# Reordering around the seams of a transformer block: masks, taps, scaled queries, readout, entry turns, tail rows

## Chip, cores and metric

The kernel runs on one core of one Trainium2 chip, as one program. The metric is the device time in microseconds, lower is better. The names of the engines are TensorE (PE, weight loads PEld), VectorE (DVE), ScalarE (ACT), GpSimd (POOL) and SyncE (SP), whose queue issues nearly all transfers.

## The reference

A transformer block on 1024 latent rows and 256 context rows of width 1024, all in float32:

```python
def _ffn_sublayer(x, shift, scale, gate, w13, w2, g, b):
    y = _swiglu(_modulate(x, shift, scale), w13, w2)
    return _layer_norm(ALPHA * x + FFN_RES * gate * y, g, b)

def reference(x, c, ctx, ...):
    ml = silu(c) @ w_ada + b_ada            # nine rows: shifts, scales, gates
    x_lat = _ffn_sublayer(x, ml[0], ml[1], ml[2], ...)
    x_ctx = _ffn_sublayer(ctx, mc[0], mc[1], mc[2], ...)
    y_lat = _token_mixer(_modulate(x_lat, ml[3], ml[4]), _modulate(x_ctx, mc[3], mc[4]), ...)
    x_lat = _layer_norm(ALPHA * x_lat + ml[5] * y_lat, ...)
    return _ffn_sublayer(x_lat, ml[6], ml[7], ml[8], ...)
```

The token mixer projects both inputs with w_in (the slices q, k, v, o and gates of an mLSTM with 4 heads of 128, and q, k, v of a banded attention with 8 heads of 64 and 2 key-value heads). q and k of the mLSTM go through a depthwise convolution of five taps and a silu. The mLSTM runs in both directions and starts from the states that the context leaves. Its result h is read out as `layer_norm_per_head(h) * g * sigmoid(o)`. The attention sees its own block and the neighbouring ones and the context, with a sink. Both results side by side are multiplied by w_out. The output is the latent rows.

## The kernel before, in words

**Products.** Each float32 operand is split into a high and a low part in the reduced format fp32r, and a product is three matmuls (high by high, low by high, high by low) that accumulate in PSUM. ScalarE makes the high part, VectorE or GpSimd the low one by a subtraction.

**Order.** Each engine's stream is written by hand, in the order of the code; engines meet at semaphores. Nothing is scheduled by a program, except that the projection's steps are cut over the attention's pairs by shares (PAIR_STEPS, below). In the order of the span: modulation and entry, the first FFN, the projection of the context and of a part of the latent rows, the mixed stage (1025 to 1305 us), the mLSTM's cores (to 1377), the output stage (to 1478), the second FFN and, in its last products, the rows of the output (to the end).

**Mixed stage.** 32 pairs of attention heads run between the steps of the projection groups 43 to 81 (mixed_pe; a step is three matmuls, a group eight steps). For a pair p TensorE turns the probabilities (L2483, after VectorE's scaling L2473), makes the next pair's scores, then this pair's values (pair_values_pe, L2505) and then the projection steps PAIR_STEPS[p]. share_cut gives each of the first 12 pairs a share of 1, the last LAST_SHARE, and the others an equal part of what is left. Before, the last pair has 17 steps and finishes groups 79, 80 and 81. In pairs 0 to 3 and 28 to 31 the probabilities are turned in two stages (turn_stages). The groups' results leave PSUM through the convolution's taps: ScalarE makes the first (L2143), VectorE the other four (L2156). After the pairs ScalarE makes the silus of k (L2169, four) and of q (L2928, four), and loads the table for it.

**Decay tiles.** The mLSTM's decays are 16 tiles of 128x512. SyncE loads a tile (L2605), GpSimd masks it (decay_mask_pool, L2636), ScalarE takes exponentials (decay_tile_act, L2628), SyncE stores it (L2611) and loads the third after it, one or two tiles a pair (decays_in). GpSimd also makes the low parts of the weights of units 6 and 7 among these masks (proj_low_pool, L2003, two instructions each) at the places in LOW_AT, and the loads of the next weights (p_raw, L1907), on SyncE's queue, wait for them.

**Cores.** TensorE runs 16 steps of 24 matmuls (L3078): eight with the state and the scaled queries q_rows, eight that update the state, eight with vext and the probabilities d_rows. SyncE loads q_rows and d_rows (rows_sp, L2800 and L2801) into six slots, row j when the last matmuls of step j-6 are done. GpSimd multiplies q_rows by the queries (scaled, L2836) and the scores by d_rows (probabilities, L2844), in the order scaled(i), probabilities(i). Ahead of the loop it makes weighted values and decayed states (weighted_pool L2886, decay_state_pool L2892), which the states of the context wait for.

**Readout.** In the last steps and behind them, for each of eight tiles: VectorE's statistics (L2975, L2982) and two small operations (L2985, L2986), GpSimd's power and product (invert_pool, L2870, L2873), ScalarE's scaling (L2922, four), GpSimd's gating (gated_pool, L2879), TensorE's turn (L3312).

**Output stage.** TensorE makes the w_out products in two halves of the columns. After tiles 5 and 6 of the second half it turns the normed rows 0 to 3 for the first product of the second FFN (L331), four of the eight column blocks each time. ScalarE reads each turn with two instructions (half_act, L358 and L360) and makes the norm of each row (norm_act, L1641). L875 is the first matmul of the second FFN.

**Tail.** The output's layer norm is made row tile by row tile, n = 0 to 7 (out_rows_dve, L3487 centring, L3495 affine). For row n = 6 only the centring is VectorE's; ScalarE scales (row_scaled_act, L3475) and GpSimd adds (L3424). ScalarE makes the sums of a row (L3447 to L3454), GpSimd the power (L3420). Of the last row VectorE makes the statistics (L3458 to L3465) after the last products' gate (L1584) and addition (L1593).

## Time and profile before

| | us |
|---|---|
| median of three runs | 2128.68 |
| the three runs | 2127.88, 2128.68, 2131.55 |
| the profiled execution's own time | 2129.62 |
| its span | 2127.8 |
| TensorE busy | 2091.4 (98%) |
| VectorE busy | 1527.0 (72%) |
| ScalarE busy | 905.6 (43%) |
| GpSimd busy | 192.8 (9%) |

The profile is one execution. The span runs from its first instruction to its last, the time has what lies around it as well. A row of a timeline is a start in us from the span's start, a length in us, the engine, the line of the kernel, the operation and its tiles, the number of instructions joined in the row, and in brackets how long the engine was idle before and what released it. Instructions of one engine are pipelined, so a row may begin before the one ahead of it ends; a matmul's end is modelled.

### The profile page before, as it was taken

Reading aid. Unit: us, or ns where it says so; the run is one execution under the profiler, and the core shown is the slowest. Engines: PE = TensorE matmul, PEld = TensorE weight load, DVE = VectorE, ACT = ScalarE, POOL = GpSimd, SP = SyncE. Lnnn points to the kernel's source line nnn. Section 1 sums busy time; section 2 is a strip of 40 time slices with the busy share of each in tenths; the row PEclk is TensorE's granted clock in tenths of the full one; section 3 lists DMA queues with packets and bytes.
Section 4 is the critical chain, followed back from the end, with each engine's and each line's share of the span. In section 5 each row is a group of like instructions: output and inputs, shape, how many; then the busy total and the mean of one; then the engine's idle time right before and its main releaser. Section 6 shows DMA issues by size and latency. Waiting matters only on the chain.

```text
span 2127.8 us, 31643 instructions
## 1 busy us (share of the span) xinstructions
PE 2091.4 (98%) x11508; PEld 1768.0 (83%) x11510; DVE 1527.0 (72%) x2520; ACT 905.6 (43%) x1631; POOL 192.8 (9%) x212
## 2 busy tenths in 40 slices
PE   8999999999999999999999999999999999999998
PEld 4888888888888888899878878877888888888886
DVE  5778888777648878675665465866867777767787
ACT  4622222222237446542565555734532323336445
POOL 0000000000000001090111002821000000000001
PEclk9999999999999999999999999999999999999999
DMA  8144444555459664733231002732244434349773
GB/s 298 33 142 147 149 134 129 160 167 159 129 186 348 193 215 148 209 101 117 74 108 41 21 21 66 182 109 99 75 134 140 136 104 153 123 139 341 257 234 112
DMA packets 261841, 310.38 MB, mean 146 GB/s; under 512 B 19350, under 2 KB 164686, under 8 KB 261710
## 3 DMA queue, kind: packets, MB, share of 16 engines
q1 hardware_dynamic: 261422, 308.52, 45.4%
q8 instruction: 80, 1.31, 0.2%
q14 instruction: 51, 0.42, 0.1%
q10 hardware_dynamic: 288, 0.13, 0.0%
HBM read 242.13 MB, written 66.45 MB: 145 GB/s over the span
## 4 chain that ended last, share of the span: by engine, by line
PE 86%; DVE 4%; DMA 3%; ACT 2%; issue 1%; POOL 1%; SPq 1%; DVEq 0%; POOLq 0%; ACTq 0%
PE psum L1327 11%; PE psum L1328 11%; PE psum L1329 11%; PE psum L1527 6%; PE psum L1529 6%; PE psum L1528 6%; PE psum L2056 3%; PE psum L2058 3%; PE psum L2057 3%; PE psum L1347 2%; PE psum L1346 2%; PE psum L1345 2%; PE psum L3078 2%; PE psum L875 2%; PE psum L876 2%; PE psum L877 2%
## 5 line engine op out<-in xcount | busy, mean ns | idle before, releaser
L1327 PE MATMUL psum<-x_mix_h,x_op_h 128*128 128x512 f32 x640 | 251.2, 393 | 1.3 <-DVE v_sum L1135 1.2
L1328 PE MATMUL psum<-x_mix_l,x_op_h 128*128 128x512 f32 x640 | 249.8, 390 | 0.0
L1329 PE MATMUL psum<-x_mix_h,x_op_l 128*128 128x512 f32 x640 | 249.5, 390 | 0.0
L1527 PE MATMUL psum<-s_high 128*128 128x512 f32 x616 | 240.0, 390 | 0.3 <-DVE s_low L1514 0.3
L1528 PE MATMUL psum<-s_low,s_high 128*128 128x512 f32 x616 | 239.9, 389 | 0.0
L1529 PE MATMUL psum<-s_high,s_low 128*128 128x512 f32 x616 | 239.9, 389 | 0.0
L1514 DVE TENSOR_TENSOR s_low<-s_raw,s_high 128x1024 fp32r<-128x1024 f32 x154 | 186.9, 1217 | 50.5 <-ACT s_high L1475 50.5
L1475 ACT ACTIVATE s_high<-s_raw 128x1024 fp32r<-128x1024 f32 x154 | 161.3, 1057 | 124.1 <-PE psum L1529 56.3
L1019 ACT ACTIVATE x_op_h<-raw 128x512 fp32r<-128x512 f32 x140 | 86.1, 627 | 203.6 <-PE psum L1329 121.1
L1019 ACT ACTIVATE x_op_h<-w_sum 128x512 fp32r<-128x512 f32 x160 | 97.1, 625 | 162.9 <-DVE w_sum L997 107.1
L1327 PEld LDWEIGHTS psum<-x_mix_h,x_op_h 128*128 128x128 f32 x640 | 120.4, 188 | 25.4 <-issue 1.8
L1329 PEld LDWEIGHTS psum<-x_mix_h,x_op_l 128*128 128x128 f32 x640 | 120.2, 188 | 25.3
L1328 PEld LDWEIGHTS psum<-x_mix_l,x_op_h 128*128 128x128 f32 x640 | 120.4, 188 | 23.2
L1527 PEld LDWEIGHTS psum<-s_high 128*128 128x128 f32 x616 | 115.7, 188 | 24.5 <-DVE s_low L1514 0.8
L1529 PEld LDWEIGHTS psum<-s_high,s_low 128*128 128x128 f32 x616 | 115.7, 188 | 24.2
L1528 PEld LDWEIGHTS psum<-s_low,s_high 128*128 128x128 f32 x616 | 115.7, 188 | 23.9
L1025 DVE TENSOR_TENSOR x_op_l<-raw,x_op_h 128x512 fp32r<-128x512 f32 x140 | 92.8, 686 | 39.2 <-ACT x_op_h L1019 37.0
L2056 PE MATMUL psum<-p_wh,xh_lat 128*128 128x256 f32 x384 | 111.7, 291 | 0.0
L2057 PE MATMUL psum<-p_wl,xh_lat 128*128 128x256 f32 x384 | 108.8, 283 | 0.0
L2058 PE MATMUL psum<-p_wh,xl_lat 128*128 128x256 f32 x384 | 108.8, 283 | 0.0
L1025 DVE TENSOR_TENSOR x_op_l<-w_sum,x_op_h 128x512 fp32r<-128x512 f32 x160 | 107.5, 683 | 0.0
L773 DVE SCALAR_TENSOR_TENSOR ada_sums<-ada_slice,more,ada_sums 128x512 f32<-128x512 f32 x140 | 99.6, 746 | 3.7 <-DVE ada_sums L773 0.5
(408 smaller groups left out, 5069.6 us busy)
## 6 DMA issues: line engine op xcount, KB each, us to landing
raw<-in_ffn_w SPq DMA_DIRECT2D x88, 512.0 KB, 5.4
f_terms<-g_half SPq DMA_DIRECT2D x154, 256.0 KB, 2.3
s_raw<-f_terms SPq DMA_DIRECT2D x154, 256.0 KB, 3.2
s_raw<-in_ffn_w SPq DMA_DIRECT2D x154, 256.0 KB, 4.0
ada_slice<-in_w_ada SPq DMA_DIRECT2D x112, 256.0 KB, 3.1
c_raw<-in_ffn_w SPq DMA_DIRECT2D x22, 512.0 KB, 3.5
p_raw<-in_w_in SPq DMA_DIRECT2D x22, 512.0 KB, 4.0
early<-in_w_ada SPq DMA_DIRECT2D x16, 512.0 KB, 6.6
```

Source lines behind the costliest of these rows:

```text
L1019: nc.scalar.activation(op_tiles(F, op)[0][:], OP_SOURCE[op], ACT.Copy).then_inc(F.hi, 1)
L1025: nc.vector.tensor_tensor(low[:], OP_SOURCE[op], high[:].bitcast(F32), ALU.subtract).then_inc(F.lo, 1)
L1327: nc.tensor.matmul(o, wh[:, k], high(k), start=i < 4 and k == 0, stop=False, skip_group_check=i > 3)
L1328: nc.tensor.matmul(o, wh[:, k], low(k), start=False, stop=False, skip_group_check=i > 3)
L1329: last = nc.tensor.matmul(o, wl[:, k], high(k), start=False, stop=k == KH - 1, skip_group_check=i > 3)
L1514: nc.vector.tensor_tensor(S.low[s % RING][:], S.raw[s % RAWS][:], S.high[s % RING][:].bitcast(F32), ALU.subtract)\
L1527: nc.tensor.matmul(o, h[:, 0, rows], h[:, 1], start=i == 0 and q in (0, 1, 6), stop=False, skip_group_check=True)
L1528: nc.tensor.matmul(o, h[:, 0, rows], l[:, 1], start=False, stop=False, skip_group_check=True)
L1529: return nc.tensor.matmul(o, l[:, 0, rows], h[:, 1], start=False, stop=i == PAIRS - 1, skip_group_check=True)
L2056: nc.tensor.matmul(o[:, 0:w], high, high_w[:, k, :], start=k == 0, stop=False)
L2057: nc.tensor.matmul(o[:, 0:w], high, low_w[:, k, :], start=False, stop=False)
L2058: last = nc.tensor.matmul(o[:, 0:w], low, high_w[:, k, :], start=False, stop=k == KD - 1)
```

## The change

- Masks: the low parts of units 6 and 7 stand one decay mask later on GpSimd (before mask 3 in place of 2, before mask 10 in place of 9).
- Last taps: LAST_SHARE is 1.75 in place of 2.5: the last pair has 12 steps and finishes groups 80 and 81; group 79 is done one pair earlier, and the five steps go to pairs 12 to 30 (pair 12 has 13 in place of 12). ScalarE makes group 79's first tap behind the first of the four silus of k, and group 80's behind the second.
- Values: in the pairs with two turn stages, two steps of the projection stand ahead of the values (three in the last, as before).
- Row loads of the cores need unit 9's group done, in place of all groups.
- Scaled queries: GpSimd scales rows 0 to 3 ahead of the loop, between the weighted values, and row i+4 behind probabilities(i).
- Readout: VectorE's two small operations (a step of its own semaphore with them) go to GpSimd, as two tensor_scalar, with one more semaphore step in front of the power.
- Entry turns: three column blocks after tile 5, three after 6, two after 7, in place of four and four after 5 and 6; so on VectorE and ScalarE, whose norms of rows 5 and 6 stand between.
- Tail: the row whose scaling and addition are ScalarE's and GpSimd's is n = 5 in place of 6; row 6 is VectorE's, and the statistics of the last row's first half are made ahead of it.

```diff
--- before.py
+++ after.py
@@ -2536,7 +2536,7 @@
...
-        FIRST_PAIRS, LAST_SHARE = 12, 2.5
+        FIRST_PAIRS, LAST_SHARE = 12, 1.75
...
@@ -2569,15 +2569,12 @@
...
                     score_pair_pe(pe, p + 1)
-                    pair_values_pe(pe, p)
...
                     pe.wait_ge(rope_kept, len(ROPED))
-                if p + 1 < ATT_PAIRS:
-                    groups_pe(pe, PAIR_STEPS[p])
-                else:
-                    groups_pe(pe, PAIR_STEPS[p][:3])
-                    pair_values_pe(pe, p)
-                    groups_pe(pe, PAIR_STEPS[p][3:])
+                ahead = 3 if p + 1 == ATT_PAIRS else 2 if len(turn_stages(p)) == 2 else 0
+                groups_pe(pe, PAIR_STEPS[p][:ahead])
+                pair_values_pe(pe, p)
+                groups_pe(pe, PAIR_STEPS[p][ahead:])
...
@@ -2669,11 +2666,13 @@
...
             keep_pair_act(act, ATT_PAIRS - 1)
-            silu_k_act(act, range(1, 3))
+            done = groups_done(ATT_PAIRS - 1)
+            silu_k_act(act, range(1, 2))
+            group_act(act, done[0])
+            silu_k_act(act, range(2, 3))
...
             silu_k_act(act, range(3, 4))
-            done = groups_done(ATT_PAIRS - 1)
-            for j in done[:-1]:
+            for j in done[1:-1]:
...
@@ -2776,8 +2775,7 @@
...
             pool.wait_ge(gate_dve, 7)
-            LOW_AT = {2: POOL_LOW[0],
-                      decays_in(next(p for p in range(ATT_PAIRS) if first_of(6) in groups_done(p))).stop: POOL_LOW[1]}
+            LOW_AT = {3: POOL_LOW[0], decays_in(HIGH_IN[POOL_LOW[1]]).stop: POOL_LOW[1]}
...
@@ -2801,7 +2799,7 @@
...
         def mlstm_sp(sp):
-            sp.wait_ge(p_ready, len(GROUPS))
+            sp.wait_ge(p_ready, unit_last(9) + 1)
...
@@ -2848,12 +2846,16 @@
...
                 weighted_pool(pool, n)
+            scaled(0)
+            scaled(1)
...
                 decay_state_pool(pool, n)
+                scaled(n)
             for i in range(LAST):
-                scaled(i)
                 probabilities(i)
+                if i + LAT0 < LAST:
+                    scaled(i + LAT0)
...
@@ -2865,11 +2867,15 @@
...
         def invert_pool(pool, q):
-            _, rate, offset = read_slots(q)
+            mv, rate, offset = read_slots(q)
+            by_head = mv.rearrange("p (h c) -> p h c", c=2)
             pool.wait_ge(read_measured, q + 1)
+            nc.gpsimd.tensor_scalar(offset, by_head[:, :, 0], -1.0, None, op0=ALU.mult)
+            nc.gpsimd.tensor_scalar(rate, by_head[:, :, 1], LN_EPS, None, op0=ALU.add).then_inc(read_inverted, 1)
+            pool.wait_ge(read_inverted, 3 * q + 1)
...
                 .then_inc(read_inverted, 1)
-            pool.wait_ge(read_inverted, 2 * q + 1)
+            pool.wait_ge(read_inverted, 3 * q + 2)
...
@@ -2916,7 +2922,7 @@
...
             _, rate, offset = read_slots(q)
-            act.wait_ge(read_inverted, 2 * q + 2)
+            act.wait_ge(read_inverted, 3 * q + 3)
...
@@ -2969,8 +2975,9 @@
...
             st = small[:, 8:32]
-            mv, rate, offset = read_slots(q)
-            by_head = mv.rearrange("p (h c) -> p h c", c=2)
+            mv, _, _ = read_slots(q)
+            if q:
+                dve.wait_ge(read_measured, q)
...
@@ -2980,11 +2987,7 @@
...
                 last = nc.vector.bn_aggr(mv[:, 2 * h:2 * h + 2], st[:, 6 * h:6 * h + 6])
-            core_step(dve, last)
-            unit = ones.to_broadcast([P, M_HEADS])
-            nc.vector.scalar_tensor_tensor(offset, by_head[:, :, 0], -1.0, unit, op0=ALU.mult, op1=ALU.mult)
-            nc.vector.scalar_tensor_tensor(rate, by_head[:, :, 1], LN_EPS, unit, op0=ALU.add, op1=ALU.mult)\
-                .then_inc(read_measured, 1)
+            last.then_inc(read_measured, 1)
...
@@ -3159,6 +3162,7 @@
...
         MIX = [(0, t) for t in TILES_BACK] + [(1, t) for t in range(TL)]
+        T3_PARTS = {5: range(3), 6: range(3, 6), 7: range(6, KD)}
...
@@ -3238,11 +3242,9 @@
...
             norm_act(act, N2, 4, 4)
-            half_act(act, F2, T3, T3_BANKS, 0, range(4))
-            norm_act(act, N2, 5, 5)
-            half_act(act, F2, T3, T3_BANKS, 0, range(4, KD))
-            norm_act(act, N2, 6, 6)
-            norm_act(act, N2, 7, 7)
+            for t in range(5, TL):
+                half_act(act, F2, T3, T3_BANKS, 0, T3_PARTS[t])
+                norm_act(act, N2, t, t)
...
@@ -3285,10 +3287,8 @@
...
                     first_low(dve, F2)
-                if (half, t) == (1, 5):
-                    half_dve(dve, F2, T3, 0, range(4))
-                if (half, t) == (1, 6):
-                    half_dve(dve, F2, T3, 0, range(4, KD))
+                if half and t in T3_PARTS:
+                    half_dve(dve, F2, T3, 0, T3_PARTS[t])
...
@@ -3363,11 +3363,8 @@
...
                 last.then_inc(mix_ready, 1)
-                if (half, t) == (1, 5):
-                    for k in range(4):
-                        turn_pe(pe, T3, T3_BANKS, norm2_done, (0, k))
-                if (half, t) == (1, 6):
-                    for k in range(4, KD):
+                if half and t in T3_PARTS:
+                    for k in T3_PARTS[t]:
...
@@ -3378,6 +3375,7 @@
...
         LAST_ROWS = list(range(4, TL)) + list(range(4))
+        SPLIT_ROW = TL - 3
...
@@ -3402,10 +3400,10 @@
...
             for n, t in enumerate(LAST_ROWS[:-1]):
-                if n < TL - 2:
-                    sp.wait_ge(out_affined, n + 1)
+                if n == SPLIT_ROW:
+                    sp.wait_ge(row_added, ADDED_BEFORE + 1)
                 else:
-                    sp.wait_ge(row_added, ADDED_BEFORE + 1)
+                    sp.wait_ge(out_affined, n + int(n < SPLIT_ROW))
...
@@ -3419,7 +3417,8 @@
...
                     .then_inc(N1.inverted, 1)
-                if n == TL - 2:
+                if n == SPLIT_ROW + 1:
+                    t = LAST_ROWS[SPLIT_ROW]
...
@@ -3469,9 +3468,9 @@
...
-            t = LAST_ROWS[TL - 2]
+            t = LAST_ROWS[SPLIT_ROW]
             act.wait_ge(row_centred, CENTRED_BEFORE + 1)
-            act.wait_ge(N1.inverted, 2 * TA + TL - 1)
+            act.wait_ge(N1.inverted, 2 * TA + SPLIT_ROW + 1)
...
@@ -3486,7 +3485,7 @@
...
                                                          op0=ALU.add, op1=ALU.mult)
-                if n == TL - 2:
+                if n == SPLIT_ROW:
...
@@ -3532,13 +3531,12 @@
...
                 if t == 3:
+                    half_sums_dve(dve, 3, 1)
...
                     out_rows_dve(dve, 4 + t - 1)
-                if t == 2:
-                    half_sums_dve(dve, 3, 1)
...
```

ScalarE at the end of the attention, from the load of the silu's table; L2169 is a silu of k, L2143 a first tap, L2928 (after the change L2934) a silu of q, L2495 and L2513 the last pair's turned probabilities and rows. Before:

```order
L2169 ACT_TABLE_LOAD
L2169 ACTIVATE kT<-kT,more 128x1280
L2495 ACTIVATE late_pT<-psum 128x512
L2495 ACTIVATE pair_pT<-psum 128x512
L2169 ACTIVATE kT<-kT,more 128x1280 x2
L2513 ACTIVATE qaT<-psum 128x128
L2169 ACTIVATE kT<-kT,more 128x1280
L2143 ACTIVATE qT<-psum,more 128x510
L2143 ACTIVATE qT<-psum,more 128x512
L2928 ACTIVATE qT<-qT,more 128x1024 x3
L2143 ACTIVATE qT<-psum,more 128x510
```

With the change:

```order
L2169 ACT_TABLE_LOAD
L2169 ACTIVATE kT<-kT,more 128x1280
L2143 ACTIVATE qT<-psum,more 128x510
L2495 ACTIVATE late_pT<-psum 128x512
L2495 ACTIVATE pair_pT<-psum 128x512
L2169 ACTIVATE kT<-kT,more 128x1280
L2143 ACTIVATE qT<-psum,more 128x512
L2169 ACTIVATE kT<-kT,more 128x1280
L2513 ACTIVATE qaT<-psum 128x128
L2169 ACTIVATE kT<-kT,more 128x1280
L2934 ACTIVATE qT<-qT,more 128x1024 x3
L2143 ACTIVATE qT<-psum,more 128x510
```

The two first taps that stood behind the fourth silu of k (groups 79 and 80) are now behind the first and the second of them. The three silus of q stand ahead of the last tap in both.

GpSimd at the start of the mLSTM's cores; w_v are weighted values, q_rows the scaled queries, d_rows the probabilities. Before:

```order
L2886 TENSOR_TENSOR w_v<-vext,tok_gate 128x516 [waits p_ready,p_read_act]
L2886 TENSOR_TENSOR w_v<-vext,tok_gate 128x516
L2886 TENSOR_TENSOR w_v<-vext,tok_gate 128x516 [waits update_ready]
L2892 TENSOR_TENSOR state<-state,decay_all 128x516 [waits state_done]
L2886 TENSOR_TENSOR w_v<-vext,tok_gate 128x516 [waits update_ready]
L2892 TENSOR_TENSOR state<-state,decay_all 128x516 [waits state_done]
L2836 TENSOR_TENSOR q_rows<-q_rows,qT 128x512 [waits silu_done,q_gate_in]
L2844 TENSOR_TENSOR d_rows<-scores,d_rows 128x512 [waits sc_kept,d_in]
L2836 TENSOR_TENSOR q_rows<-q_rows,qT 128x512 [waits rope_in]
L2844 TENSOR_TENSOR d_rows<-scores,d_rows 128x512 [waits gate_in]
```

With the change:

```order
L2892 TENSOR_TENSOR w_v<-vext,tok_gate 128x516 [waits p_ready,p_read_act]
L2892 TENSOR_TENSOR w_v<-vext,tok_gate 128x516
L2834 TENSOR_TENSOR q_rows<-q_rows,qT 128x512 [waits silu_done,q_gate_in]
L2834 TENSOR_TENSOR q_rows<-q_rows,qT 128x512 [waits rope_in]
L2892 TENSOR_TENSOR w_v<-vext,tok_gate 128x516 [waits update_ready]
L2898 TENSOR_TENSOR state<-state,decay_all 128x516 [waits state_done]
L2834 TENSOR_TENSOR q_rows<-q_rows,qT 128x512 [waits q_gate_in]
L2892 TENSOR_TENSOR w_v<-vext,tok_gate 128x516 [waits update_ready]
L2898 TENSOR_TENSOR state<-state,decay_all 128x516 [waits state_done]
L2834 TENSOR_TENSOR q_rows<-q_rows,qT 128x512 [waits rope_in]
L2842 TENSOR_TENSOR d_rows<-scores,d_rows 128x512 [waits sc_kept,d_in]
L2834 TENSOR_TENSOR q_rows<-q_rows,qT 128x512 [waits q_gate_in]
```

Four scaled rows moved ahead of the first probabilities; from then on a row is scaled four steps before its own probabilities.

VectorE in the tail, from the centring of row 5; L1584 and L1593 are gate and addition of a 512-wide product, L3458 (L3457) statistics of half a row. Before:

```order
L3487 SCALAR_TENSOR_TENSOR y<-y,out_stats,ln_rows_286 128x1024
L3495 SCALAR_TENSOR_TENSOR y<-y,out_stats,ln_rows_286 128x1024
L3458 BN_STATS out_stats<-y 128x6
L3487 SCALAR_TENSOR_TENSOR y<-y,out_stats,ln_rows_286 128x1024
L1584 TENSOR_TENSOR s_sums<-psum,gate_row_278 128x512
L1593 SCALAR_TENSOR_TENSOR y<-y,s_sums 128x512
L3458 BN_STATS out_stats<-y 128x6
```

With the change:

```order
L3486 SCALAR_TENSOR_TENSOR y<-y,out_stats,ln_rows_286 128x1024
L3457 BN_STATS out_stats<-y 128x6
L3486 SCALAR_TENSOR_TENSOR y<-y,out_stats,ln_rows_286 128x1024
L3494 SCALAR_TENSOR_TENSOR y<-y,out_stats,ln_rows_286 128x1024
L1584 TENSOR_TENSOR s_sums<-psum,gate_row_278 128x512
L1593 SCALAR_TENSOR_TENSOR y<-y,s_sums 128x512
L3457 BN_STATS out_stats<-y 128x6
```

Of row 5 only the centring is left here, the statistics moved ahead of row 6, and row 6 has both its instructions ahead of the last gate.

## Rows read from the trace of the kernel before

**Rows 1.** The page's part 1: busy us, share of the span, instructions.
```profile
PE 2091.4 (98%) x11508; PEld 1768.0 (83%) x11510; DVE 1527.0 (72%) x2520; ACT 905.6 (43%) x1631; POOL 192.8 (9%) x212
```

**Rows 2.** Waits of TensorE, 1000 to 1500 us: total, times, longest.
```profile
PE psum L2483 <- DVE att_p L2473: 6.4, 5, 3.2
...
PE psum L3312 <- POOL y_m L2879: 1.2, 2, 0.6
...
PE psum L331 <- ACT x_quarter L360: 0.9, 2, 0.7
...
PE psum L2505 <- ACT pair_pT L2495: 0.6, 2, 0.3
```

**Rows 3.** Windows: length, busy time by engine, granted clock, DMA share, bandwidth.
```profile
1090.00:1100.00 10.00, 6.81 (x52) 5.05 (x51) 4.79 (x10) 4.99 (x15) 2.29 (x3) 1.00 0.64 184
...
1300.00:1310.00 10.00, 8.01 (x29) 6.13 (x28) 6.00 (x8) 6.02 (x8) 0.00 (x0) 0.83 0.00 0
...
1360.00:1375.00 15.00, 11.11 (x83) 10.76 (x81) 13.58 (x44) 9.01 (x27) 12.08 (x13) 0.89 0.15 41
```

**Rows 4.** Timelines by unit 7: start, length, engine, line, operation, idle time before.
```profile
1086.78 4.75 POOL L2003 TENSOR_TENSOR p_wl<-p_raw,p_wh 128x1024 fp32r<-128x1024 f32 x2 [10.20 <-ACT p_wh L1985]
...
1089.19 2.73 SPq L1907 DMA_DIRECT2D p_raw<-in_w_in  x2
...
1095.81 1.31 PE L2483 MATMUL psum<-ident,att_p 128*128 128x128 f32 x10 [3.19 <-DVE att_p L2473]
...
1100.49 1.28 ACT L2628 ACTIVATE d_stage<-d_stage,tok_gate 128x128 f32<-128x128 f32 x4 [2.69 <-POOL d_stage L2636]
```

**Rows 5.** Timelines of GpSimd and TensorE by unit 6.
```profile
1040.45 4.73 POOL L2003 TENSOR_TENSOR p_wl<-p_raw,p_wh 128x1024 fp32r<-128x1024 f32 x2 [9.20 <-ACT p_wh L1985]
...
1057.92 1.09 PE L2483 MATMUL psum<-ident,att_p 128*128 128x128 f32 x8 [1.50 <-DVE att_p L2473]
```

**Rows 6.** Timelines of ScalarE and TensorE, end of attention.
```profile
1304.15 3.21 ACT L2928 ACTIVATE qT<-qT,more 128x1024 f32<-128x1024 f32 x3
...
1305.52 0.59 PE L2047 MATMUL psum<-xh_lat,p_wh 128*128 128x512 f32 x1 [1.99 <-DVE qT L2156]
...
1318.04 1.16 PE L3063 MATMUL psum<-qT,kT 128*128 128x128 f32 x8 [0.30 <-ACT qT L2928]
```

**Rows 7.** Loop: timelines, a window of TensorE, landings of q_rows.
```profile
1359.92 3.55 DVE L2985 SCALAR_TENSOR_TENSOR small<-small,consts 128x4 f32<-128x4 f32 x1
...
1362.18 1.27 POOL L2844 TENSOR_TENSOR d_rows<-scores,d_rows 128x512 f32<-128x512 f32 x1
...
1365.89 1.13 PE L3078 MATMUL psum<-state,q_rows 128*128 128x129 f32 x8 [3.81 <-issue]
...
1375.20 1.13 PE L3078 MATMUL psum<-state,q_rows 128*128 128x129 f32 x8 [0.28 <-issue]
...
1340.00:1360.00 20.00, 19.68 (x175) 19.52 (x176) 1.00 0.93 241
...
DMA to landing us min/median/max: 3.5/4.3/5.9
```

**Rows 8.** Timeline of GpSimd, readout.
```profile
1403.00 0.20 POOL L2873 TENSOR_TENSOR small<-small 128x4 f32<-128x4 f32 x1
...
1404.97 1.29 POOL L2879 TENSOR_TENSOR y_m<-y_m,o_in 128x512 f32<-128x512 f32 x1 [1.77 <-ACT y_m L2922]
```

**Rows 9.** Timelines of ScalarE and TensorE, entry turns.
```profile
1478.28 1.32 ACT L1641 ACTIVATE y<-y,ln_stats 128x1024 f32<-128x1024 f32 x1
...
1478.52 0.50 PE L875 MATMUL psum<-xh_lat,f_h 128*128 128x512 f32 x1 [0.37 <-ACT x_quarter L360]
```

**Rows 10.** Timelines of VectorE and GpSimd, tail.
```profile
2119.24 0.69 DVE L1593 SCALAR_TENSOR_TENSOR y<-y,s_sums 128x512 f32<-128x512 f32 x1
...
2121.18 2.28 DVE L3487 SCALAR_TENSOR_TENSOR y<-y,out_stats,ln_rows 128x512 f32<-128x512 f32 x2
...
2119.51 2.62 POOL L3424 TENSOR_TENSOR y<-y,ln_rows 128x1024 f32<-128x1024 f32 x1 [2.15 <-ACT y L3475]
```

## The prediction, made before the changed kernel ran

> **What bounds the kernel now.** I began with the page: TensorE is busy for 98% of the span [rows 1], so only its pauses, its slow clock and what stands ahead of its first and behind its last matmul can give or cost time. Next the waits of TensorE from 1000 to 1500 us [rows 2], where all of the change but its last part lies: 6.4 us before the turns L2483, 1.2 before L3312, 0.9 before L331, 0.6 before L2505; a pause of 3.81 in the mLSTM loop, put down to no releaser, comes on top [rows 7]. Then the granted clock [rows 3]: 1.00 at 1090 to 1100, although a pause of 3.19 us lies in it; 0.83 at 1300 to 1310; 0.89 at 1360 to 1375. Ten us at 0.83 lack 1.7 us of work at 2.4 GHz, fifteen at 0.89 also 1.7. Each of these two falls to 1.2 GHz lies about a pause (1.99 and 3.81 us, [rows 6, 7]). Then the timelines of the four engines at each place.
>
> **The sum** is made against the profiled execution: span 2127.80, its own time 2129.62. The median of the runs is 2128.68, 0.94 lower, so 0.94 is taken off at the end.
>
> **A. Mask ahead of the low parts of unit 6: 0.** GpSimd sat idle 9.20 us before that low part, released by ScalarE's high part at 1040.45 [rows 5]. One mask more ahead of it finds its rows not yet loaded or an idle engine. The low part still waits for ScalarE, and the pause of 1.50 behind it stays.
>
> **B. The same for unit 7: -0.3.** Before: GpSimd's low parts take 4.75 us from 1086.78, the mask stands behind them, ScalarE's decay exponentials, queued ahead of the softmax, come late, and TensorE waits 3.19 at 1095.81 [rows 4]. With the mask first this pause goes. But SyncE issues the decay tile's store and the next load behind p_raw's two loads, which wait for the low parts (2.73 us from 1089.19). That queue isn't changed: the next tile's mask still waits for a load, so its exponentials (they stood 2.69 us idle at 1100.49 [rows 4]) come late one pair further on. Behind that pair TensorE waits about 2.9 instead of 3.19. Bounds: -3.2 (no pause returns) and +1.7 (the same pause, with a fall of the clock).
>
> **C. Last taps, LAST_SHARE 1.75: -3.9.** At 1305.52 TensorE waits 1.99 for VectorE's taps [rows 6], and these wait for ScalarE's first tap, which stood behind all four silus of kT. Now that tap stands behind one silu, the next behind two, and group 79 is done a pair earlier: the pause goes (-2.0), and with it the fall of the clock in that stretch (-1.7). The five steps that leave the last pair fill others: of the five pauses at L2483 (6.4), those of 3.19 and 1.50 leave 1.7 for three, and larger pairs lie at two of these: -0.9. Against it: the three silus of qT (3.21 us [rows 6]) now stand right ahead of group 81's tap on ScalarE, which comes about 1 us later as the group is done sooner after them; the wait of 0.30 for the last silu at 1318.04 becomes 1.0: +0.7. Bounds -4.7 and -2.0.
>
> **D. Values two steps later in seven pairs: +0.4.** The two pauses it aims at are 0.6 together [rows 2]. They lie in pairs 0 and 1, ahead of the 1.50 of A, which is set by a chain of GpSimd and ScalarE: what is saved ahead of it is waited for there. What stays is one more switch between projection and values in each pair. Bounds 0 and +1.0.
>
> **E. Scaled queries four ahead, small operations off VectorE: -4.0.** TensorE's longest pause, 3.81 at 1365.89, has VectorE's L2985 as its cause: an operation on 128x4 elements that took 3.55 us while GpSimd ran its instructions of 1.27 us without a gap [rows 7]. L2985 is gone: -3.8, and the fall of clock behind it, -1.7. What it costs: GpSimd now runs probabilities(i+1) behind scaled(i+4), which needs row i+4. SyncE issues that row when the matmuls of step i-2 are done. A step has 24 matmuls and 175 ran in 20 us [rows 7]: 2.7 a step. From there to the start of step i+1's last 8 matmuls are 3 x 2.7 - 1.0 = 7.1 us; two GpSimd instructions, 2.5, leave 4.6 for the row's landing. The rows land in 3.5 to 5.9, 4.3 in the middle [rows 7]; the long ones are those of the loop's start, where weights load beside them. Before, the same scaling had five steps. Writing the loop out step by step with these numbers, its end moves from 1375.6 (clock at 2.4 GHz throughout) to 1371.9 with all landings at 3.5, 1372.6 at 4.3, 1374.7 at 5.1, 1377.9 at 5.9. I take 1373.1, since one or two rows will be late and the others not: against the profile (the last step begins at 1375.20 [rows 7] and ends 1.9 later, 1377.1) -4.0. Bounds -5.2 and +0.8.
> The row says that one VectorE instruction waited for three of GpSimd in a row. The Trainium skill (SBUF — State Buffer, Who interferes with whom) has an exclusive lock for a VectorE instruction with two SBUF inputs against a GpSimd instruction that reads SBUF, held by the first to issue for its whole instruction; by that the wait would be one instruction, 1.2, and E would bring 2.4 less, since the rest of the 3.81 would have another cause. The trace disagrees with it in length: 3.55 is nearly three times 1.27.
>
> **F. Readout: +1.2.** Two tensor_scalar of 128x4 and one more semaphore step now stand on GpSimd in the chain statistics, power, product, ScalarE, gating. TensorE waited for the end of that chain (1.2 at L3312 [rows 2]), and so did GpSimd for ScalarE (1.77 before the last gating [rows 8]), so the chain's length counts whole. A 128x4 product there takes 0.20 [rows 8]; two of them and a step more, less the two that leave VectorE, I put at 0.4 a tile over the last three tiles. Bounds 0.6 and 1.8.
>
> **G. Entry turns in threes: +1.0.** ScalarE's two last parts went on until L875 at 1478.52; the norm of row 6 came behind them, 1.32 from 1478.28 [rows 9]. It now stands ahead of the last two turns: +1.3, and the second FFN starts so much later. Of the 0.9 at L331 [rows 2] 0.3 goes. Bounds 0 and 1.8. TensorE's idle time gathers in one piece of about 3 us ahead of L875, a place where the clock may fall.
>
> **H. Tail: +1.5.** Before, row 6's addition on GpSimd (2.62 from 2119.51) held VectorE's L3487: two halves 2.28, of which 1.4 is their work, and the last L3495 began right behind it, at 2123.5 [rows 10]. Now row 5 goes to GpSimd, and its addition comes when ScalarE has scaled it, which it does after the sums of row 6: about 2117.95. VectorE is then in row 6's L3495 (until about 2118.8, as it must wait for its power). GpSimd's addition follows, 2118.8 to 2121.2, and VectorE's L1593, two SBUF inputs, which was at 2119.24, gets held until 2121.2: +2.0. The 0.9 of holding at L3487 is gone, the last power now comes up while L3487 holds the way: +0.1 to +0.7. Bounds +0.3 (the two never meet) and +2.6 (GpSimd gets in first, row 6's L3495 waits for it, and PSUM-reading L1584 too).
> The Trainium skill (SBUF — State Buffer, Who interferes with whom) says that a VectorE instruction with one SBUF input doesn't contend; by that L1584 passes. No row above shows it, and the sum holds both.
>
> Sum: 0 - 0.3 - 3.9 + 0.4 - 4.0 + 1.2 + 1.0 + 1.5 = -4.1. There are three places with a new or remaining pause of 1.3 to 3 us (turns of the pair behind unit 7, loop start, ahead of L875). A pause of 1.99 had a fall and one of 3.19 had none, so the pause alone doesn't decide; I expect one fall, +1.7. 2129.62 - 4.1 + 1.7 - 0.94 = **2126.3**.
>
> **Rivals.**
> 1. *The gains stand, no fall* (chance 0.25). For: both falls of before lie at pauses that go. 2126.3 - 1.7 = 2124.6; with landings at 3.5 to 4.3 (-0.9) and a harmless tail (-1.2) 2122.5.
> 2. *Unit 7's pause doesn't return* (0.10): the store after unit 7 finds the queue free early enough. 2126.3 - 2.9 = 2123.4.
> 3. *The row's landing becomes the loop's bound, slower* (0.14). At 1329 to 1339 weights, rows and gates load together, and the landing of 5.9 is from there. The point is 4.6; from it each us costs some 4. With 5.9 throughout, +4.8: 2131.1; with the several pauses in one stretch a second fall, +1.7: 2132.8; with the tail at its worst, +1.1: 2133.9. Against: rows later in the loop landed in 3.5 to 4.3.
> 4. *Two or more falls* in the new pauses (0.06): 2128.1 to 2129.9.
> The change does what it says in the order of the instructions, so no rival is made of that.
>
> **Numbers.** The forecast has 0.45, with its own range 2124.4 to 2129. About 0.2% (4.3 us) is what a measurement can tell from no change: 2124.4 to 2132.9. Faster: rivals 1 and 2, and 0.03 of the forecast, 0.38. Slower: two thirds of rival 3, 0.10. The rest, 0.52, is within. The range reaches from rivals 1 and 2 with a part of the low bounds, 2120.5, to rival 3, 2132.5.
>
> **What will show it.** B: a wait of about 2.9 before L2483 at 1101 to 1104 and none at 1096. C: no wait before L2047 near 1304, clock 1.00 there, a wait of about 1 before L3063. E: no L2985; the waits of TensorE in the loop's first eight steps, behind L2842 (probabilities), and q_rows' landings against 4.6. F: the gatings of the last tiles 0.4 further apart on GpSimd. G: the norm of row 6 ahead of the last two turns, L875 about 1.3 later behind row 5's norm, idle in one piece. H: VectorE's L1593 held until GpSimd's addition ends. I am wrong if the loop's end, counted from its first L3078, doesn't come at least 2 us earlier, or if a part that I cost at nothing (A) shows a pause.

## The result

The changed kernel takes **2141.86 us** (median of five runs, 2138.93 to 2144.56), the kernel before 2129.17 in the same comparison. One of the five runs of before took 4236.48 us; the ratio is made without it. The ratio is 1.0059, 95% interval 1.0047 to 1.0070: slower by 12.6 us. The forecast was 2126.3, its range 2120.5 to 2132.5; the chance given to a loss was 0.10.

The profiled execution of the changed kernel took 2142.53 us, its span is 2140.4. I cut both spans at the starts of eight rows that both traces have, and take the differences:

| stage, from one start to the next | before | changed | difference |
|---|---|---|---|
| up to the first turn L2483 of the mixed stage (not edited) | 1031.8 | 1030.0 | -1.8 |
| mixed: to the scores' wait (L3063, now L3066) | 286.2 | 283.5 | -2.7 |
| cores: to their last eight matmuls (L3078, now L3081) | 58.1 | 62.0 | +3.9 |
| readout: to the turn of tiles 5 to 7 (L3312) | 30.2 | 37.8 | +7.6 |
| output stage: to L875 | 72.1 | 74.5 | +2.4 |
| second FFN: to the last matmul | 639.6 | 640.8 | +1.3 |
| tail: to the last affine operation (L3495, now L3494) | 5.4 | 7.7 | +2.3 |
| its outputs | 4.3 | 3.9 | -0.4 |

**Profile after.** TensorE's part of the page, and its waits from 1000 to 1500 us, which answer to [rows 1, 2]:

```profile
PE 2096.9 (98%) x11508; PEld 1773.2 (83%) x11510; DVE 1524.0 (71%) x2504; ACT 907.1 (42%) x1631; POOL 197.9 (9%) x228
...
PE psum L3312 <- POOL y_m L2885: 5.9, 2, 3.5
PE psum L3081 <- POOL d_rows L2842: 5.7, 3, 2.6
PE psum L2483 <- DVE att_p L2473: 5.0, 3, 2.7
PE psum L875 <- ACT x_quarter L360: 3.3, 1, 3.3
...
PE psum L3066 <- ACT qT L2934: 1.2, 1, 1.2
```

The share is still 98%, and nothing in the page tells of a loss of 12 us; the waits do. L3312 went from 1.2 us to 5.9, the loop's matmuls wait 5.7 for probabilities, and one pause of 3.3 stands ahead of L875. Of the waits of before, those at L2505, L331 and L2047 are gone.

The windows around the pauses (length, busy times, granted clock, DMA share, GB/s), which answer to [rows 3]:

```profile
1100.00:1110.00 10.00, 7.25 (x48) 5.72 (x48) 7.00 (x13) 7.79 (x24) 1.27 (x2) 0.83 0.43 139
1330.00:1345.00 15.00, 12.47 (x97) 12.28 (x96) 9.72 (x23) 11.59 (x35) 11.59 (x9) 0.89 0.76 209
1352.00:1367.00 15.00, 11.89 (x89) 11.70 (x90) 9.21 (x36) 8.97 (x30) 11.39 (x10) 0.89 0.46 135
1385.00:1395.00 10.00, 7.61 (x40) 6.72 (x39) 3.70 (x18) 5.13 (x12) 3.50 (x7) 0.83 0.15 47
1408.00:1420.00 12.00, 8.47 (x39) 6.82 (x37) 6.23 (x11) 6.76 (x11) 3.25 (x5) 0.86 0.33 86
1485.00:1495.00 10.00, 7.10 (x24) 5.71 (x25) 3.86 (x9) 4.09 (x6) 1.13 (x2) 0.83 0.26 105
```

Each of the six stretches has a fall to 1.2 GHz: 10 us at 0.83, 12 at 0.86 and 15 at 0.89 lack 1.7 us each, the same step as before. With one near 40 us there are seven before the last matmul; the profile of before has three (near 40 too, and the two of [rows 3]). Between these two executions four more falls of 1.7 are 6.8 of the 12.6 us. Over all runs it is less. The mean granted clock was 0.9934 in the five runs of the changed kernel and 0.9950 in the 64 runs of the kernel before that were made beside the experiments, which lack 14.1 and 10.7 us. By that estimate 3 of the 12.6 us are clock, about two falls; the profile of before was one with few.

### The profile page after: what moved, and what is told of

Its sections match the earlier page's. It is cut to its first block, busy times and chain, and to the rows that moved or that the text cites. A ratio compares the mean times of both kernels' runs of the same rounds, so it can differ in the third digit from the quotient of the medians.

```text
span 2140.4 us, 31650 instructions
## 1 busy us (share of the span) xinstructions
PE 2096.9 (98%) x11508; PEld 1773.2 (83%) x11510; DVE 1524.0 (71%) x2504; ACT 907.1 (42%) x1631; POOL 197.9 (9%) x228
## 4 chain that ended last, share of the span: by engine, by line
PE 89%; DMA 3%; POOL 2%; ACT 2%; DVE 2%; issue 1%; SPq 1%; DVEq 0%; POOLq 0%; ACTq 0%
PE psum L1328 12%; PE psum L1327 12%; PE psum L1329 12%; PE psum L1527 6%; PE psum L1529 6%; PE psum L1528 6%; PE psum L2056 3%; PE psum L2058 3%; PE psum L2057 3%; PE psum L1347 2%; PE psum L1346 2%; PE psum L1345 2%; PE psum L875 2%; PE psum L876 2%; PE psum L877 2%; PE psum L2483 1%
## 5 line engine op out<-in xcount | busy, mean ns | idle before, releaser
L1634 POOL TENSOR_TENSOR ln_stats<-ln_stats,consts 128x1 f32<-128x1 f32 x18 | 15.5, 863 | 950.8 <-DVE ln_stats L1629 950.8
```

## The experiments

Each kernel's stages, cut as above, in us of its profiled execution, and its median and ratio to the kernel before with the 95% interval:

| kernel | mixed | cores | readout | output | FFN | tail | median | ratio |
|---|---|---|---|---|---|---|---|---|
| before | 286.2 | 58.1 | 30.2 | 72.1 | 639.6 | 5.4 | 2129.2 | |
| changed | 283.5 | 62.0 | 37.8 | 74.5 | 640.8 | 7.7 | 2141.9 | 1.0059 [1.0047, 1.0070] |
| e1 | 285.9 | 56.4 | 34.4 | 74.6 | 639.2 | 7.7 | 2135.5 | 1.0031 [1.0019, 1.0042] |
| e2 | 285.7 | 61.9 | 30.4 | 73.8 | 640.8 | 7.7 | 2137.9 | 1.0039 [1.0025, 1.0052] |
| e3 | 285.3 | 61.1 | 37.4 | 72.7 | 639.6 | 7.7 | 2141.7 | 1.0062 [1.0045, 1.0079] |
| e4 | 286.1 | 60.8 | 37.8 | 74.6 | 640.8 | 5.4 | 2140.5 | 1.0054 [1.0034, 1.0075] |
| e5 | 285.3 | 59.2 | 36.2 | 73.8 | 640.6 | 7.8 | 2140.5 | 1.0057 [1.0040, 1.0073] |
| e6 | 286.7 | 60.9 | 36.2 | 75.7 | 639.3 | 7.7 | 2139.5 | 1.0045 [1.0029, 1.0062] |
| e7 | 284.4 | 59.1 | 30.3 | 72.1 | 639.6 | 5.4 | 2127.4 | 0.9994 [0.9985, 1.0004] |
| e8 | 286.0 | 58.1 | 30.8 | 72.2 | 640.0 | 5.4 | 2128.9 | 0.9998 [0.9989, 1.0008] |
| e9 | 286.1 | 58.1 | 30.2 | 72.2 | 639.6 | 5.4 | 2127.1 | 0.9987 [0.9978, 0.9997] |
| e10 | 284.0 | 54.2 | 31.2 | 72.1 | 639.7 | 5.4 | 2121.9 | 0.9961 [0.9948, 0.9974] |
| e11 | 285.5 | 55.4 | 37.5 | 74.3 | 640.8 | 7.7 | 2137.9 | 1.0038 [1.0026, 1.0050] |
| e12 | 285.3 | 60.4 | 36.1 | 75.7 | 639.2 | 7.8 | 2141.4 | 1.0061 [1.0043, 1.0078] |
| e13 (one run) | 285.0 | 55.7 | 31.1 | 72.1 | 639.6 | 5.4 | 2125.0 | |
| e14 | 285.2 | 54.1 | 31.1 | 72.1 | 639.6 | 5.4 | 2124.1 | 0.9973 [0.9962, 0.9985] |
| e15 | 282.9 | 54.3 | 30.9 | 72.1 | 639.7 | 5.4 | 2120.6 | 0.9964 [0.9950, 0.9978] |

Runs of one kernel lie 2 to 10 us apart, so an edit of 2 us is read from its stage, not from the medians.

**e1: scaled queries not ahead.**

```diff
-            scaled(0)
-            scaled(1)
...
-                scaled(n)
             for i in range(LAST):
+                scaled(i)
                 probabilities(i)
-                if i + LAT0 < LAST:
-                    scaled(i + LAT0)
```

> The changed kernel with GpSimd's order in the cores as before: scaled(i) right ahead of probabilities(i), none four ahead. Measured from the first score matmul (L3066) to the start of the last eight matmuls of the cores this stage took 58.1 us before and 62.0 with the change. Theory (the row's landing became the loop's bound, since probabilities(i+1) stands behind the scaling of row i+4): the three waits for probabilities (2.5, 0.5, 2.6) and the fall of the clock behind them go, and since VectorE's L2985 is no longer there either, the stage takes 53 to 55 and the whole time falls by 7 to 9 us against the changed kernel (2141.9). Rival (SyncE's queue and the load beside it: the rows are loaded earlier, so the weights' loads fall differently): the order on GpSimd doesn't matter, the stage stays at 60 to 63.

The cores take 56.4, 5.6 less than in the changed kernel, and the median falls by 6.3. The waits for probabilities are gone, so the theory's mechanism holds and the rival (60 to 63) does not; the theory's sizes, 53 to 55 and 7 to 9 us, were both missed. What is missing is a new wait, for scaled queries at 1370, where GpSimd's longer readout operations stand ahead of them, with a fall of the clock at it:

```profile
1370.08 2.06 PE L3077 MATMUL psum<-state,q_rows 128*128 128x129 f32 x8 [2.68 <-POOL q_rows L2834]
```

The changed kernel's rows show what e1 took away. GpSimd, SyncE's queue, TensorE and the landings of q_rows:

```profile
1334.12 1.27 POOL L2834 TENSOR_TENSOR q_rows<-q_rows,qT 128x512 f32<-128x512 f32 x1 [3.35 <-DMA q_rows<-gate_rows]
...
1355.51 1.27 POOL L2834 TENSOR_TENSOR q_rows<-q_rows,qT 128x512 f32<-128x512 f32 x1 [3.07 <-DMA q_rows<-gate_rows]
...
1327.63 1.76 SPq L1913 DMA_DIRECT2D p_raw<-in_w_out  x2
1329.50 0.54 SPq L2798 DMA_DIRECT2D q_rows<-gate_rows  x1
...
1346.40 1.28 SPq L1913 DMA_DIRECT2D p_raw<-in_w_out  x2
1347.78 0.54 SPq L2798 DMA_DIRECT2D q_rows<-gate_rows  x1
...
1336.67 1.16 PE L3081 MATMUL psum<-vext,d_rows 128*128 128x129 f32 x8 [2.53 <-POOL d_rows L2842]
...
1358.05 1.66 PE L3081 MATMUL psum<-vext,d_rows 128*128 128x129 f32 x8 [2.62 <-POOL d_rows L2842]
...
DMA to landing us min/median/max: 3.5/4.0/7.7
```

Two rows of the ten that are issued in the loop do most of it, and both stand right behind loads of weights (p_raw) on SyncE's queue. Row 6 could have gone when step 0's last matmul ended, at 1327.0, but is issued at 1329.50 and lands 4.5 later: 7.0 in all against the budget of 4.6, and TensorE waits 2.53. Row 12 is issued at 1347.78, 0.3 after its slot was free, and lands 7.7 later, the longest landing. GpSimd, with the probabilities of an earlier step queued behind it, stands idle 3.07 and scales it at 1355.51, and TensorE waits 2.62. This is rival 3, down to its budget. The six other kernels that scale four ahead (e2 to e6, e12) repeat it: row 6 stands behind weights in all of them, and TensorE waits 2.0 to 2.7 us there; row 12 lands 6.0 to 7.9 after its issue.

**e2: the readout's small operations on VectorE again.**

```diff
-            nc.gpsimd.tensor_scalar(offset, by_head[:, :, 0], -1.0, None, op0=ALU.mult)
-            nc.gpsimd.tensor_scalar(rate, by_head[:, :, 1], LN_EPS, None, op0=ALU.add).then_inc(read_inverted, 1)
-            pool.wait_ge(read_inverted, 3 * q + 1)
...
+            core_step(dve, last)
+            nc.vector.scalar_tensor_tensor(offset, by_head[:, :, 0], -1.0, unit, op0=ALU.mult, op1=ALU.mult)
+            nc.vector.scalar_tensor_tensor(rate, by_head[:, :, 1], LN_EPS, unit, op0=ALU.add, op1=ALU.mult)
```

> The changed kernel with the two small operations of the readout on VectorE again (two scalar_tensor_tensor behind a step), GpSimd having power and product alone. From the start of the last eight matmuls of the cores to the last turn of the readout (L3312, 12 matmuls) it took 30.2 us before and 37.8 with the change. Theory (each of eight tiles has two more GpSimd operations and a semaphore round in a chain that TensorE waits for, 0.7 to 1.2 us a tile, and the late third tile delays ScalarE's gate rows and with them the next): this stage falls to 30 to 32, with 1 to 2.5 us on top in TensorE's clock. In the cores' stage L2985 is back and may again stand behind GpSimd's instructions for 1 to 3.6 us, so that of the 6 to 7 us up to 3.6 are lost there. Rival (the readout is late because the cores end late and ScalarE's other work stands in the way): the stage stays above 35.

The readout takes 30.4 in place of 37.8: theory. The median falls by 4.0 only; 1.7 of the 7.4 is a fall of the clock that this profile of the changed kernel has in the stage. The chain of one tile in the changed kernel, on GpSimd:

```profile
1400.57 1.30 POOL L2885 TENSOR_TENSOR y_m<-y_m,o_in 128x512 f32<-128x512 f32 x1 [1.77 <-ACT y_m L2928]
1401.95 0.56 POOL L2873 TENSOR_SCALAR small<-small 128x4 f32<-128x4 f32 x1
1402.57 0.53 POOL L2874 TENSOR_SCALAR small<-small 128x4 f32<-128x4 f32 x1
1403.19 1.04 POOL L2876 TENSOR_TENSOR small<-small,consts 128x4 f32<-128x4 f32 x1
1404.30 0.20 POOL L2879 TENSOR_TENSOR small<-small 128x4 f32<-128x4 f32 x1
1406.27 1.29 POOL L2885 TENSOR_TENSOR y_m<-y_m,o_in 128x512 f32<-128x512 f32 x1 [1.77 <-ACT y_m L2928]
```

From gating to gating it is 5.70 us; before, the same two gatings were 4.75 apart (1400.22 to 1404.97, the later one in [rows 8]). The two tensor_scalar take 0.56 and 0.53 while VectorE runs its low parts, and 0.23 each at 1388.7 to 1389.3, where VectorE is idle. L2985 (L2987 in this kernel) met no row of GpSimd's instructions (it took 0.16 to 0.88); the order on GpSimd is another here, which is likely the reason; the loss of 1 to 3.6 us in the cores that I allowed for did not come, and the cores' 61.9 are e1's matter.

**e3: entry turns in fours**, T3_PARTS = {5: range(4), 6: range(4, KD)} and ScalarE's order with it.

> The changed kernel with the entry turns in fours again. From the last readout turn to L875 it took 72.1 us before and 74.5 with the change, and the first 12 us of the second FFN ran at a granted clock of 0.86. Theory (the norm of row 6 ahead of the last two turns on ScalarE makes one idle stretch of 3.3 us, and the clock falls behind it): the pause before L875 falls from 3.3 to 0.4 to 0.6, the clock behind it is 1.00, and the time falls by 2.5 to 4.5 us against the changed kernel. Rival (the pause only gathers what lies at other places otherwise): L331 gets its 0.9 back and two thirds of the gain are gone, below 1.5 us.

The pause before L875 is gone (changed: 3.27 at 1487.90, with a clock of 0.83 behind it in the window above), the output stage is 1.8 shorter and the FFN 1.2: 3.0 us by the profile, as the theory has it. The median moved by 0.2 only, which is the rival's size. The four runs had a lower clock on average, 0.9922 against 0.9934, which is 2.5 us, so the medians don't decide. Nor is the 3.0 all certain: eight profiles have the pause of 3.3 (3.25 to 3.27), and a fall stands behind it in five (changed, e2, e4, e5, e11) and not in e1, e6 and e12.

**e4: the tail as before**, SPLIT_ROW = TL - 2, the half's statistics back in their place.

> The changed kernel with the tail as before: row 6 is the one that is scaled by ScalarE and added by GpSimd. From the last matmul to the last affine operation (L3494) it took 5.4 us before and 7.7 with the change, in which row 6's L3494 took 3.3 us beside GpSimd's addition. Theory: the stage is 5.4 again, 2.3 us less. Rival (the delay came from elsewhere, as from ScalarE's sums being later): it stays above 7.

5.4 again: theory. What the exchange did, VectorE and GpSimd in the changed kernel:

```profile
2129.03 3.28 DVE L3494 SCALAR_TENSOR_TENSOR y<-y,out_stats,ln_rows 128x1024 f32<-128x1024 f32 x1 [0.50 <-POOL out_stats L3418]
2132.23 0.68 DVE L1584 TENSOR_TENSOR s_sums<-psum,gate_row 128x512 f32<-128x512 f32 x1
2132.94 0.69 DVE L1593 SCALAR_TENSOR_TENSOR y<-y,s_sums 128x512 f32<-128x512 f32 x1
...
2134.89 1.54 DVE L3486 SCALAR_TENSOR_TENSOR y<-y,out_stats,ln_rows 128x512 f32<-128x512 f32 x2
...
2127.45 1.47 POOL L3418 TENSOR_TENSOR out_stats<-out_stats,consts 128x1 f32<-128x1 f32 x1 [5.08 <-ACT out_stats L3453]
2128.89 2.34 POOL L3423 TENSOR_TENSOR y<-y,ln_rows 128x1024 f32<-128x1024 f32 x1
```

GpSimd's addition and VectorE's L3494 both want to start at 2129, as both come behind the power L3418; GpSimd goes first (2.34 us), L3494 takes 3.28 in place of the 1.28 of a row of that size, and everything behind it, the last gate L1584 first, is 2 us late. L3486 of the last row gets 0.7 back (1.54 in place of 2.28 [rows 10]).

**e5: masks as before**, LOW_AT with 2 and 9.

> The changed kernel with only the masks' places as before (low parts of units 6 and 7 ahead of masks 2 and 9). From the first turn of the mixed stage to the first scores of the last head (the wait for silu of q) the kernel before took 286.2 us; the changed kernel and four variants of it took 283.5 to 286.1, all with a wait of 2.6 to 2.8 near 1102 and matmuls at half the clock behind it. Theory (the pause only moved, and at its new place the clock falls, which it did not before): with the masks back the pause is 3.2 near 1094 again, the clock there is 1.00, and the stage takes 282 to 283.5. Rival (the masks' move changes nothing by itself; the clock falls there because of the values' or shares' move): the stage stays at 284.5 to 286, with a granted clock below 1.00 between 1090 and 1110.

The pause is 3.20 at 1096.46 again and the clock there is 1.00, but a fall stands near 1058 in its place, at the pause behind unit 6's masks, which nobody touched. The stage is 285.3, within the rival's bounds and outside the theory's. Neither holds: this pointed to chance, which e13 then tested.

**e6: values as before**, the two steps ahead of them only in the last pair.

> The changed kernel with the values right behind the next pair's scores again in pairs 0 to 3 and 28 to 30. Theory (switches of 0.4 in all, swallowed or not): the mixed stage changes by less than 1 us (284 to 286). Rival (in these pairs the values two steps later delay ScalarE's copy of the pair's rows and so the turns): 1 to 3 us less, 282 to 283.5.

286.7 with three falls (5.1). Without pauses (the scores' wait among them) and falls the stage has a rest of 273.2 us, against 275.1 in the changed kernel. The ten profiles with the values moved have 274.7 to 275.2, the seven without 273.1 to 273.7. (The figures up to 276.4 in the expectation of e9 left the scores' wait in.) TensorE in pair 28 of the changed kernel, from two steps to values and back:

```profile
1283.22 0.50 PE L2047 MATMUL psum<-xh_lat,p_wh 128*128 128x512 f32 x1
1283.56 0.40 PE L2048 MATMUL psum<-xl_lat,p_wh 128*128 128x512 f32 x1
...
1284.50 0.39 PE L2049 MATMUL psum<-xh_lat,p_wl 128*128 128x512 f32 x1
1284.82 0.66 PE L2505 MATMUL psum<-pair_pT,va 128*64 128x128 f32 x8
...
1285.85 0.50 PE L2047 MATMUL psum<-xh_lat,p_wh 128*128 128x512 f32 x1
1286.18 0.40 PE L2048 MATMUL psum<-xl_lat,p_wh 128*128 128x512 f32 x1
```

Matmuls of a projection start 0.23 apart. Behind a switch it is 0.34 (1283.22 to 1283.56), ahead of the values 0.32. No pause is shown for it. Pairs 28, 29 and 30 lasted 8.21, 7.53 and 8.22 from turn to turn, and 7.96, 7.27 and 7.95 here: 0.26 a pair, 1.8 for seven. The theory said less than 1 and the rival 1 to 3 by a later copy; the rest moves by 1.9, the rival's size by another way. The stage as a whole, 286.7, is outside both ranges because of its three falls.

**e7: the attention's parts alone**, all behind it as before.

> The kernel before with the attention's parts alone: masks, LAST_SHARE with the last taps, values; rows, scaled queries, readout, entry turns and tail as before. Theory (the loss of 12 us lies in cores, readout, entry and tail): the mixed stage as in the changed kernel (283.5 to 286), cores 58, readout 30 and tail 5.4 as before, so the time is 2127 to 2130. Rival (the last taps' new order makes the scores' wait of 1.2 and carries it into the cores): the cores' stage is 1 to 2 us longer than 58.1 and the time is 2130 to 2132.

2127.4, readout and tail as before. The cores' one microsecond more is in the clock: behind the same pause of 3.81 (now at 1361) 3.4 us are lost, not 1.7. The loss of 12 us lies in cores, readout, entry and tail.

**e8: e7 with one-input operations.**

```diff
-            nc.vector.scalar_tensor_tensor(offset, by_head[:, :, 0], -1.0, unit, op0=ALU.mult, op1=ALU.mult)
+            nc.vector.tensor_scalar(offset, by_head[:, :, 0], -1.0, None, op0=ALU.mult)
```

> The same, and the two small operations of the readout, on VectorE, are tensor_scalar with one SBUF input (mean by -1, variance plus epsilon) in place of scalar_tensor_tensor with a second input of ones. Theory (the 3.55 us of L2985 came from its second SBUF input, which goes through what GpSimd holds): the operation takes 0.2 to 0.3, the pause of 3.8 in the cores and the clock's fall behind it go, cores 53 to 55 in place of 58, time 2122 to 2126. Rival (any VectorE operation that reads SBUF waits there while GpSimd runs without a gap): the pause stays at 2.5 to 3.8 and the time is that of the kernel with the attention's parts alone.

```profile
1359.26 3.54 DVE L2982 TENSOR_SCALAR small<-small 128x4 f32<-128x4 f32 x1
```

The rival's pause and time hold: tensor_scalar with one input waits as long as the form with two. Its reason, that any operation reading SBUF waits there, is what e10 tests.

**e9: last taps alone**, LAST_SHARE 1.75 and ScalarE's taps on the kernel before.

> The kernel before with LAST_SHARE 1.75 and ScalarE's last taps moved, nothing else (masks, values and all behind the attention as before). The mixed stage, from the first turn to the scores' wait, was 286.2 us before: pauses 10.8, a fall of the clock 1.75, and 273.7 in which TensorE ran without a pause that the profile shows. With the values two steps later that rest was 274.7 to 276.4 in six kernels, with them back 273.2. Theory (the last taps gain what was forecast, and the values' move gives 2 us back that no pause shows): rest 273 to 274, pauses 7 to 8.5, no fall or one, the stage 281 to 283.5; the time 2124 to 2127. Rival (the rest grows because the five steps lie in larger pairs): rest 275 to 276, stage 284 to 285, time 2127 to 2129.

Rest 273.1, pauses 7.9 in place of 10.8, as the theory has it, but three falls in this execution (5.1), and the stage 286.1, outside both ranges. The median, over ten runs, is 2.4 lower and the interval excludes 1. The wait for the last silu of q is 1.19 in place of 0.30.

**e10: e9 with reductions.**

```diff
+            mv = small[:, at:at + 12].rearrange("p (h c) -> p h c", c=3)
...
-            nc.vector.scalar_tensor_tensor(offset, by_head[:, :, 0], -1.0, unit, op0=ALU.mult, op1=ALU.mult)
-            nc.vector.scalar_tensor_tensor(rate, by_head[:, :, 1], LN_EPS, unit, op0=ALU.add, op1=ALU.mult)
+            nc.vector.reduce_sum(rate, mv[:, :, 1:3], AX_X)
+            nc.vector.reduce_max(offset, mv[:, :, 0:1], AX_X, negate=True)
```

> As e9, and the two small operations of the readout on VectorE are reductions: the negated mean as a maximum over one element, variance plus epsilon as a sum over two neighbouring elements (epsilon is written into the slots once). Both have one SBUF input, and neither is a tensor_scalar. Theory (L2985 waited 3.55 us for GpSimd because of the way it reads, as scalar_tensor_tensor and as tensor_scalar; the statistics around it, which are reductions, never waited): the reductions take 0.15 to 0.3, TensorE's pause of 3.8 in the cores and the fall behind it go, cores 52.5 to 54.5 in place of 58.1, 3.5 to 5.5 us less than e9. Rival (whichever instruction comes first after the statistics waits there): the first reduction takes 3.5 and the cores stay at 58.

VectorE and TensorE at the place where L2985 took 3.55:

```profile
1355.44 0.16 DVE L2982 TENSOR_REDUCE small<-small 128x4 f32<-128x8 f32 x1
1355.52 0.15 DVE L2983 TENSOR_REDUCE small<-small 128x4 f32<-128x4 f32 x1
...
1366.57 1.13 PE L3076 MATMUL psum<-state,q_rows 128*128 128x129 f32 x8 [0.60 <-POOL q_rows L2834]
```

0.16 and 0.15. The pause and the fall are gone, the cores take 54.2, and the time is 2121.9: 5.3 under e9, 0.4% under the kernel before, 20 us under the changed one. So an operation that reads SBUF doesn't have to wait there.

**e11: queries two ahead.** Only scaled(0) and scaled(1) ahead of the loop, scaled(i + 2) in it.

> The changed kernel with the queries scaled two ahead in place of four: rows 0 and 1 between the weighted values, scaled(i+2) behind probabilities(i). The row that stands ahead of probabilities(i+1) is then i+2, issued two steps (5.4 us) earlier. Theory (a row's landing against a budget of 4.6 us): with 10 us of budget every landing fits, the waits for probabilities go, cores 53 to 57 in place of 59.2 to 62.0. Rival (the second landing of the pair or the weights on SyncE's queue delay the rows by more than 5 us): a wait of more than 1 us for probabilities stays.

No wait for probabilities is left, cores 55.4 against 62.0: the budget is the point, as with e1. A pause of 2.22 near 1370, behind the readout's operations, stays.

**e12: row loads wait for the last group.**

> The changed kernel with SyncE's row loads of the cores waiting for the last group again, four ahead kept. Theory (only rows from the seventh on are late, and these go by the matmuls of step i-2): cores as in the changed kernel, 59 to 62. The first four rows would land 4 to 6 us after the last group, so if the early loads matter, GpSimd's first scaling comes late and the states with it: 1 to 4 us more, 62 to 66.

60.4, as in the changed kernel: the early loads are worth nothing and cost nothing, and the late landings aren't theirs.

**e13: the kernel before once more.**

> The kernel before, unchanged. Theory (the falls of the clock at pauses of 1.5 to 3.2 us come by chance): the mixed stage shows a clock loss other than 1.75 us, or falls at other places than 1302, as near 1058 or 1096; its rest is 273 to 274. Rival (they belong to the change's order): one fall again, at the pause near 1304, none at 1058 and 1096, stage 286.2 +- 0.3.

```profile
1090.00:1100.00 10.00, 6.87 (x44) 5.03 (x45) 5.63 (x11) 6.72 (x21) 0.63 (x1) 0.83 0.52 155
1300.00:1310.00 10.00, 8.01 (x41) 6.43 (x40) 6.11 (x9) 4.74 (x7) 0.81 (x1) 1.00 0.00 0
...
1356.13 1.09 DVE L2985 SCALAR_TENSOR_TENSOR small<-small,consts 128x4 f32<-128x4 f32 x1
1357.14 1.30 DVE L2986 SCALAR_TENSOR_TENSOR small<-small,consts 128x4 f32<-128x4 f32 x1
...
1357.15 1.27 POOL L2836 TENSOR_TENSOR q_rows<-q_rows,qT 128x512 f32<-128x512 f32 x1
...
1360.79 1.13 PE L3078 MATMUL psum<-state,q_rows 128*128 128x129 f32 x8 [2.49 <-issue]
```

The theory holds, and further than I meant. The pauses are the same to 0.01 us (3.19, 1.99), but the clock fell at the first (0.83) and not at the second (1.00), the opposite of [rows 3]. And L2985, 3.55 in the first profile, took 1.09 here. L2986 behind it, 0.15 in the first, took 1.30: each of the two ends as one of GpSimd's instructions does (at 1357.2 and 1358.4), where L2985 alone had waited for three. The pause behind them is 2.49 with no fall. The span is 4.7 shorter.

**e14: reductions alone** on the kernel before; **e15: e10 with two ahead.**

> The kernel before with the readout's two small operations as reductions, nothing else. Theory: cores 54 in place of 58.1, the readout's stage 30 to 31, all else as before, 2124 to 2126. Rival (the gain of e10 needs the last taps' order as well): cores 56 or more, 2127 to 2129.

> As e10 (last taps and reductions), with the queries scaled two ahead. In e10 one wait of 0.6 for scaled queries is left in the cores (54.2). Theory (a wait for scaled queries behind the readout's power and product on GpSimd goes; landings have 10 us): cores 53.0 to 53.8, time the same as e10 within its spread (2120 to 2123). Rival (in the last steps the order puts scaled rows ahead of probabilities that TensorE waits for): cores 55 or more.

e14: cores 54.1, ratio 0.9973: the gain doesn't need the taps. Of the 5.9 us by which its median is lower, about 4 are clock by the same estimate as above: 0.9965 on average against 0.9946 in the 14 runs of before beside it. e15: cores 54.3, no better than e10. The theory's 53.0 to 53.8 was missed, the rival's 55 too. Scaling two ahead gained nothing here, and 2120.6 is the same time as e10's within the intervals.

## Why the prediction was wrong

**A, masks of unit 6: right.** That pause is still there, 1.78 us (before 1.50).

**B, masks of unit 7: the pause right in mechanism and size, the clock not.** The forecast was a pause of 2.9 between 1101 and 1104:

```profile
1098.43 0.64 POOL L2633 TENSOR_SCALAR_AFFINE_SELECT d_stage<-d_stage 128x512 f32<-128x512 f32 x1 [8.29 <-DMA d_stage<-gate_rows]
1099.11 1.28 ACT L2625 ACTIVATE d_stage<-d_stage,tok_gate 128x128 f32<-128x128 f32 x4 [5.89 <-POOL d_stage L2633]
1102.78 1.54 PE L2483 MATMUL psum<-ident,att_p 128*128 128x128 f32 x6 [2.75 <-DVE att_p L2473]
```

A wait further on the queue gave it back: the mask waited for its load, ScalarE's exponentials for the mask. The fall behind it isn't the new place's alone, as e13 has one behind the old one. But the two places don't fare alike. All ten profiles with the masks moved have falls there, 3.1 us on average; of the seven with the pause at its old place (3.19 to 3.21) two have none, and the average is 1.7. So the move may have cost 1.4 us of clock, with a forecast of -0.3; other edits differ between these kernels, and it isn't tested by itself.

**C, last taps: the mechanism right, -3.9 too large.** The pause of 1.99 went, some of the small ones too (idle time in the mixed stage 10.8 to 7.9 in e9), and the scores' wait rose to 1.2, forecast 1.0. But the 1.7 for the fall at 1304 was no property of that pause: e13 and e14 have the pause without the fall. Ten runs of e9 give -2.4, close to the -2.2 that the forecast is without it.

**D, values: mis-sized.** +0.4 with a bound of 1.0 stood there; it is 1.9. The switches cost 0.26 a pair in spacing, and no view of waits lists it.

**E, the cores: the step that failed** (-4.0 against +3.9). L2985 went as forecast. I named the budget of 4.6 us for a row's landing and the slope beyond it, and then took a few late rows at 1373.1, a gain of 4.0. What the working left out is SyncE's queue: it has a row issued as soon as its slot is free, and row 6 went out 2.5 us after that.

In the changed kernel GpSimd stood idle 0.5 to 3.4 us for a row at five steps, TensorE waited 2.53, 0.51 and 2.62, and two of the pauses brought a fall. The stage grew by 3.9 (rival 3, which had a chance of 0.14). The median landing, 4.0, is even shorter than before; the longest, 7.7, and the order of SyncE's queue decide. A median against a limit told nothing: GpSimd waited for five of the ten rows issued in the loop, TensorE in three places, and that was enough. The size has some chance in it: two falls are 3.4 of the 62.0, the kernel before has one in its 58.1, and in the six other kernels that scale four ahead the stage takes 59.2 to 61.9.

**F, the readout: the second step that failed,** +1.2 against +7.6. Three things were mis-sized. A tile's period rose by 0.95, not 0.4, since the small operations on GpSimd are twice as long beside VectorE's work and one more semaphore step stands between them. It counts in all tiles of the chain, not in the last three: the gating that the first turn waits for ends 2.4 later in the span (pause 2.39 at 1388.78, before 0.64), ScalarE's gate rows stand behind that turn, and the next readout behind them. And both pauses brought falls, 3.4, of which the second lies in the output stage. In e6 and e12, without a whole fall inside it, the stage still takes 36.2 and 36.1.

**G, entry turns: mis-sized,** +1.0 against 3.0 (e3), of which the fall comes in five of eight profiles. The pause of 3.3 was forecast as "about 3 in one piece"; I counted 1.3 of it, taking the rest as gathered from elsewhere, and left the fall to a general allowance.

**H, the tail: the size within its bounds by luck,** +1.5 against +2.3. The case that I summed, GpSimd's addition behind row 6's L3494 and holding L1593, didn't come. GpSimd got in first, the case of the upper bound, and L3494 was held: the addition stands right behind the power L3418 on GpSimd, and L3494 waits for the same power, so both became ready as it ended. The passing of L1584 isn't tested, since VectorE's own queue held it.

**The clock.** I allowed one new fall at +1.7 for three pauses, and let two old ones go for certain. The changed kernel's profile has seven against three; by the mean clocks of all runs it is about two more. A pause of 2 to 4 us has a chance of a fall, so it carries more than its own length: the one of 3.2 near 1094 has falls in five of seven profiles, the one of 3.3 ahead of L875 in five of eight, the one of 1.99 in one of three. Between the first profile of before (falls near 40, 1306 and 1367) and e13 (one near 1094) four places of falls differ with the same instructions. The falls' price was right; treating each as a property of its pause was not.

What e1 to e4 give back in their stages is 5.6 + 7.4 + 3.0 + 2.3 = 18.3 us; by the medians it is 6.3 + 4.0 + 0.2 + 1.3 = 11.8, and the changed kernel is 14.4 over e7, which has none of the four. The profile of the changed kernel, with its seven falls, makes the stages look dearer than the runs do. The four stages of the table above are 3.9 + 7.6 + 3.7 + 2.3 = 17.5 longer than before, and the start, which no edit touches, the mixed stage and the outputs 4.9 shorter: 12.6. The 1.7 by which e1's cores are shorter than those of before fits L2985's part, won by the change and lost again; it isn't tested by itself.

**What VectorE waits for.** The Trainium skill (SBUF — State Buffer, Who interferes with whom) says that tensor_reduce never contends on trn2, and that tensor_scalar can, when it enters a two-port mode. The runs agree: 0.16 for the reduction (e10), 3.54 for tensor_scalar (e8), though no trace shows whether it was in that mode. That the loser waits for one whole instruction only, as I weighed it at E, is what e13 shows, where L2985 and L2986 each waited for one (1.09 and 1.30), and not what the first profile shows, where L2985 waited 3.55 over three of them. Why the two executions differ is open.

## To carry to other kernels

Where an engine works without a gap, don't ask which engine is less busy but which operations it shares a way with: here a form that VectorE runs without waiting gave 5 to 6 us by the medians, while moving the work to GpSimd cost 4 by the medians and 7 in the profile. When an operation is moved ahead in a queue, compare what it waits for with the slowest landing, not with the median, count what stands ahead of the load on its own queue, and price what is then queued behind it. And a pause of some microseconds ahead of TensorE costs its length and, some of the time, a fall of the clock of 1.7 us; two profiles of the same kernel tell how much of a difference is that.

## What I had not expected of the hardware

The same kernel had its falls of the clock at other pauses in a second execution, with pauses equal to 0.01 us (3.19 and 1.99). A VectorE instruction on 128x4 elements waited for 3.55 us, nearly three GpSimd instructions of 1.27, in one execution and for 1.09 in the other, where the instruction behind it waited 1.30. A projection's matmul behind a switch from attention starts 0.34 us after the first in place of 0.23, which appears in no wait.
